# Attention with the keys on partitions, four heads in one product, in a two-layer hybrid trunk

## What is computed

```python
ATT_HEADS, ATT_KV_HEADS, HEAD_DIM, PAST_LEN, DEC_SEQ, SEQ = 8, 2, 64, 256, 1024, 128
# latent tokens see 256 cached keys and the 1024 latent keys; context tokens see their own 128
k_all = concatenate([ctx_k, k]); v_all = concatenate([ctx_v, v])
q = q.reshape(B, T, KV, G, HD) * HEAD_DIM ** -0.5
s = einsum('bqkgd,bskd->bkgqs', qblk, k)
p = softmax(s, axis=-1)
o = einsum('bkgqs,bskd->bqkgd', p, v)
```

## Time and profile before

| | |
|---|---|
| median of three runs | 3227.2 us |
| span of the profiled execution | 3228.9 us |
| latent attention, from its first product to the first of the context stage | 573.6 to 876.8 us |
| context attention, to the first instruction of the output projection | 876.8 to 901.2 us |
| PE busy | 2992.1 us, 93% of the span |
| VectorE, ScalarE, POOL busy | 66%, 39%, 40% |

### The profile page before, as it was taken

One profiled execution on the slowest core, in us unless ns is written; L12 is line 12 of the kernel. 1 busy time (PEld: TensorE's weight loads), 2 busy tenths in 40 slices (PEclk: granted clock), 3 DMA queues, 4 the chain that ended last, 5 costly groups with the idle time before them and its releaser, 6 DMA issues.

```text
span 3228.9 us, 44484 instructions
## 1 busy us (share of the span) xinstructions
PE 2992.1 (93%) x17516; PEld 2613.0 (81%) x17516; DVE 2128.0 (66%) x2691; ACT 1245.2 (39%) x2037; POOL 1278.3 (40%) x851
## 2 busy tenths in 40 slices
PE   7999878999889999999999899959889999999998
PEld 3898657899768999988877888747678999978876
DVE  3689578555467744468796646479777644378886
ACT  2311146555454323233323476544353332233322
POOL 1211036100022544468881221146442544478870
PEclk9999989999989999999999999966799999999999
DMA  5466644100022232243333333242132223232341
GB/s 208 159 248 209 202 134 134 37 25 1 11 98 92 74 111 91 91 140 111 111 114 104 112 116 103 89 126 60 48 103 80 97 91 104 94 131 97 111 170 59
DMA packets 230815, 347.01 MB, mean 107 GB/s; under 512 B 32040, under 2 KB 124240, under 8 KB 230608
## 3 DMA queue, kind: packets, MB, share of 16 engines
q1 hardware_dynamic: 230608, 344.17, 32.0%
HBM read 259.18 MB, written 84.94 MB: 107 GB/s over the span
## 4 chain that ended last, share of the span: by engine, by line
PE 67%; DVE 13%; POOL 10%; issue 4%; ACT 3%; DMA 2%; SPq 1%; POOLq 0%; DVEq 0%; ACTq 0%
PE psum L979 18%; PE psum L1171 9%; PE psum L656 8%; POOL d_slot L1111 5%; PE psum L2462 4%; PE psum L659 4%; PE psum L1276 3%; PE psum L1624 3%; PE psum L2450 2%; PE psum L2457 2%; PE psum L2762 2%; PE psum L1153 2%; DVE mix_x L2945 1%; PE psum L426 1%; PE psum L3689 1%
## 5 line engine op out<-in xcount | busy, mean ns | idle before, releaser
L1171 PE MATMUL psum<-d_slot 128*128 128x512 f32 x2016 | 465.0, 390 | 11.8 <-DVE yacc L1216 6.9
L1171 PEld LDWEIGHTS psum<-d_slot 128*128 128x128 f32 x2016 | 377.5, 188 | 95.0 <-DVE yacc L1216 8.6
L979 PE MATMUL psum<-AT,w_slot 128*128 128x288 f32 x2688 | 366.0, 295 | 4.7 <-POOL w_slot L944 4.7
L979 PEld LDWEIGHTS psum<-AT,w_slot 128*128 128x128 f32 x2688 | 359.5, 188 | 5.1 <-POOL w_slot L944 5.1
L1111 POOL TENSOR_TENSOR d_slot<-down_a,d_slot 128x512 fp32r<-128x512 f32 x168 | 300.4, 1811 | 71.8 <-ACT d_slot L1102 71.6
L591 POOL TENSOR_TENSOR WT<-RAW,WT 128x1024 fp32r<-128x1024 f32 (+3 forms) x34 | 115.1, 3411 | 457.8 <-ACT WT L580 457.8
L656 PE MATMUL psum<-WT,AT 128*128 128x512 f32 (+1 forms) x1296 | 280.6, 377 | 4.2 <-ACT stage L702 4.2
L979 PE MATMUL psum<-s_hi,w_slot 128*128 128x288 f32 x1344 | 269.1, 295 | 5.9 <-issue 4.3
L656 PEld LDWEIGHTS psum<-WT,AT 128*128 128x128 f32 x1296 | 230.6, 189 | 47.1 <-ACT stage L702 4.4
L944 POOL TENSOR_TENSOR w_slot<-RAW,w_slot 128x512 fp32r<-128x512 f32 x112 | 155.8, 1402 | 224.2 <-ACT w_slot L940 224.2
L979 PEld LDWEIGHTS psum<-s_hi,w_slot 128*128 128x128 f32 x1344 | 215.4, 188 | 7.1 <-issue 5.2
(11 more groups left out here) (431 smaller groups left out, 6093.3 us busy)
## 6 DMA issues: line engine op xcount, KB each, us to landing
RAW<-ffn_w SPq DMA_DIRECT2D x40, 1024.0 KB, 6.4
ada_raw<-ada_w SPq DMA_DIRECT2D x36, 1024.0 KB, 6.4
hidden<-hid SPq DMA_DIRECT2D x56, 576.0 KB, 3.3
down_a<-hidden SPq DMA_DIRECT2D x48, 512.0 KB, 6.4
RAW<-ffn_w SPq DMA_DIRECT2D x48, 512.0 KB, 7.8
RAW<-w_in_even SPq DMA_DIRECT2D x5, 2048.0 KB, 8.1
RAW<-w_in_odd SPq DMA_DIRECT2D x5, 2048.0 KB, 7.8
mix_x<-x_all SPq DMA_DIRECT2D x18, 512.0 KB, 3.5
```

What stands on the lines that cost most here:

```text
L979: mm = nc.tensor.matmul(psum[:, bank + b, 0:HB], w_slot[p][:, w, k, :], TOKENS[p][x][:, k, b * HB:(b + 1) * HB], start=(begins and k == 0 ...
L1171: mm = nc.tensor.matmul(psum[:, D_RING[q % 3] + pair % 2, :], slot[:, 0, x, k, pair * P:(pair + 1) * P], slot[:, 1, w, k, :], start=(k == ...
```

## The change

The unit of work becomes a batch: one query tile and the four heads that share a key head, so 16 latent batches and two context ones, and both attention stages become one.

- Row maxima are taken as before, but from scores that leave out the low part of k (`scores`, L2517 of the changed file). The negated maxima are turned and repeated over partitions by a transpose (`turn_maxima`, L2523), and kept in `m_q`, partitions 64 to 127, with the high part of q beside them (POOL, L2683). The low part of `kS` now has a row of ones (and zeros) in its upper half, so that the second product of `turned_scores` adds low k by high q and subtracts the maximum.
- Scores are made again with the keys on partitions (`turned_scores`, L2538 and L2539), two one-pass products of 512 columns (four heads of 128 queries) for each of ten key tiles. ScalarE takes exponentials of those; nothing is turned.
- Values times probabilities (`values`) is 512 columns wide. In four of ten key tiles it is one float32 product (L2556). In six ScalarE takes the exponential twice, into float32 and into fp32r (L2598, L2601), POOL subtracts (L2696), and three one-pass products follow (L2552 to L2554). The values carry 64 columns of ones, so that partitions 64 to 127 of the result are the sums. ScalarE inverts the sums by Ln and Exp (L2608, L2609); VectorE multiplies (`out`).
- `BEHIND` is 2: PE issues the values of step s-2 after the turned scores of step s. A step is one key tile.
- The POOL part of weight group 6 moves to batches 10 to 13, and the loads of the next stage are issued when the last turned scores are done.
- In the mLSTM stage POOL splits only one copy of the low part of k, and there are a few memsets; semaphores are regrouped into three sets.

```diff
@@ mlqk_gpsimd
-                nc.gpsimd.tensor_tensor(hl_k(qk_hl, s, 1), rot_k, hl_k(hlf, s, 0), ALU.subtract).then_inc(qk_split, 1)
+                nc.gpsimd.tensor_tensor(hl_k(qk_hl, s, 1)[:, :, 0, :], qk_rot[:, 8:10, :, :].rearrange("p h c n -> p h (c n)"), hl_k(hlf, s, 0)[:, :, 0, :], ALU.subtract).then_inc(qk_split, 1)
...
+            for s in range(2):
+                for h in (9, 11):
+                    nc.gpsimd.memset(hlf[:, s, h, HD:P], 0.0).then_inc(one_row, 1)
...
@@ att_tensor
-            for n in range(UNITS):
...
-                turn(n, 0, 6)
...
-                    values(n - 1)
...
+            def turned_scores(n, kt):
...
+                if s >= 3:
+                    pe.wait_ge(exp_done, s - 2)
...
+                nc.tensor.matmul(out, kS[:, g, 0, at:at + P], qS[:, g::2, t * P:(t + 1) * P], start=True, stop=False)
+                nc.tensor.matmul(out, kS[:, g, 1, at:at + P], per_head(m_q[:, m_slot(n), :]), start=False, stop=True).then_inc(st_done, 1)
+
+            def values(s):
...
+                pe.wait_ge(exp_done, s + 1)
...
+                if is_split(s):
+                    i, j = SPLIT.index(kt), splits_to(s) % 2
+                    pe.wait_ge(low_done, splits_to(s) + 1)
+                    nc.tensor.matmul(psum[:, o_bank(n), :], values_hl[:, i, g, 0:P], p_high[:, j, :], start=(kt == 0), stop=False)
+                    nc.tensor.matmul(psum[0:HD, o_bank(n), :], values_hl[:, i, g, P:P + HD], p_high[:, j, :], start=False, stop=False, skip_group_check=True)
+                    nc.tensor.matmul(psum[:, o_bank(n), :], values_hl[:, i, g, 0:P], p_low[:, j, :], start=False, stop=False).then_inc(pv_done, 1)
+                    return
...
+                    turned_scores(n, kt)
+                    if n < 2 * CTX - 1:
+                        if kt in (1, 3, 5, 7):
+                            scores(n + 1, kt // 2)
...
+                    if s >= BEHIND:
+                        values(s - BEHIND)
...
+            gate_tensor(pe, 0, 0, diag_att, bank=0)
@@ att_scalar
+            def exponent(s):
+                act.wait_ge(st_done, s + 1)
+                if s >= 3:
+                    act.wait_ge(pv_done, s - 2)
+                if is_split(s):
+                    nc.scalar.activation(prob[:, s % 3, :], psum[:, st_bank(s), :], ACT.Exp)
+                    if splits_to(s) >= 2:
+                        act.wait_ge(pv_done, SPLIT_STEPS[splits_to(s) - 2] + 1)
+                    nc.scalar.activation(p_high[:, splits_to(s) % 2, :], psum[:, st_bank(s), :], ACT.Exp).then_inc(exp_done, 1)
+                    return
...
+                    exponent(steps_to(n) + kt)
+                    if kt == 3 and n:
+                        inverse(n - 1)
+                    if kt == 6 and 4 <= n < 8:
+                        split_high(act, 6, (n - 4, 4))
@@ att_vector
+                    biggest(n, 0)
+                    biggest(n, 1)
+                    if n >= 2:
+                        out(n - 2)
+                    biggest(n, 2)
+                    biggest(n, 3)
@@ att_gpsimd
+                    for kt in SPLIT[:3]:
+                        low(steps_to(n - 1) + kt)
+                copy_queries(n)
+                leave(n - 2)
+                if 10 <= n < 14:
...
+                    ins = nc.gpsimd.tensor_tensor(WT[:, 0, 1, part], RAW[:, part], WTf[:, 0, 0, part], ALU.subtract)
...
+                    for kt in SPLIT[3:]:
+                        low(steps_to(n - 1) + kt)
```

More of the change, by code:

```diff
@@ new lines, in trunk, with batch, key_tiles, steps_to @@
+        BATCHES = 2 * TILES
+        LAST = BATCHES - 1
+        kSf_, qSf = kS[:].bitcast(F32), qS[:].bitcast(F32)
+        per_head = lambda a: a.rearrange("p (j n) -> p j n", j=4)
+        per_pair = lambda a: a.rearrange("p (b r n) -> p b r n", b=2, r=2)
+        def batch(n):
+            return n // 2, n % 2
+        def key_tiles(n):
+            return 1 if n // 2 == CTX else KT
+        def steps_to(n):
+            return sum(key_tiles(m) for m in range(n))
+        def maxima_to(n):
+            return 4 * min(n, 2 * CTX) + max(0, n - 2 * CTX)
@@ new lines, in step_of, with is_split, splits_to @@
+        def step_of(s):
+            n = next(n for n in range(BATCHES) if s < steps_to(n + 1))
+            return n, s - steps_to(n)
+        ALL_STEPS = steps_to(BATCHES)
+        BEHIND = 2
+        SPLIT = [kt for kt in range(KT) if kt % 5 in (0, 2, 3)]
+        WHOLE = [kt for kt in range(KT) if kt not in SPLIT]
+        def is_split(s):
+            n, kt = step_of(s)
+            return n // 2 != CTX and kt in SPLIT
+        SPLIT_STEPS = [s for s in range(ALL_STEPS) if is_split(s)]
+        def splits_to(s):
+            return sum(1 for r in SPLIT_STEPS if r < s)
@@ L3757, in mixer_sync @@
                 att_sync(sp)
-                next_stage(sp, "latent attention")
-                ctx_sync(sp)
-                next_stage(sp, "context attention")
+                next_stage(sp, "attention")
             else:
@@ L3787, in mixer_scalar @@
                 next_stage(act, "mLSTM chunks and norms")
-                att_scalar(act)
-                next_stage(act, "latent attention")
-                ctx_scalar(act)
-                next_stage(act, "context attention")
+                att_scalar(act, chain)
+                next_stage(act, "attention")
             else:
@@ L3819, in mixer_vector @@
                 next_stage(dve, "mLSTM chunks and norms")
-                att_vector(dve, chain)
-                next_stage(dve, "latent attention")
-                ctx_vector(dve, chain)
-                next_stage(dve, "context attention")
+                att_vector(dve)
+                next_stage(dve, "attention")
             else:
```

445 lines of the change are left out of this document (212 added, 233 removed).

## The result

The changed kernel takes 3177.1 us by the median of four runs (3175.9 to 3178.2), against 3228.6 for the kernel before in four (3225.1 to 3231.9). The ratio is 0.9837, with a 95% interval of 0.9825 to 0.9849: 1.6% faster. Between the medians lie 51.5 us. The forecast was 3175.0, within 3158 to 3202. The profiled execution of the changed kernel took 3175.9 with a span of 3174.2.

What follows compares the result with a forecast made beforehand. PE was taken to bound the latent attention. The terms 238 + 3 + 9.5 + 8 + 4 + 6.5 + 7 gave 276 us for what took 327.6, saving 52 from 3227.2: 3175 us, range 3158 to 3202.

Steps and rivals of the forecast that it cites:

- Batches in steady state: Sixteen latent batches: PE work of 14.9 us each, 238 us, plus 0.2 us lost a batch, 3 us.
- The path of the split steps: From turned score over ScalarE and POOL to values: 2.9 us, against 2.7 to 3.6 us of PE cover.
- Weight pieces: POOL's four pieces of weight group 6, batches 10 to 13: each lands nearly whole on PE, 9.5 us, ends 4 to 12.
- Start and clock: Stage start: 8 us before turned scores can flow, and 4 us for PE work at half clock until 586 to 590.
- Context batches and end: Two context batches with a wait for the result bank, 6.5 us, then 7 us of gate tail to the barrier.
- mLSTM stage: Extra semaphore clears and memsets, a narrower low part of k: nothing to half a microsecond either way.
- After the stage: Behind the attention stage nothing was counted; the saving of 52 us was taken from the median of 3227.2.
- The signs: Traces to check: batches 15.0 to 15.2 us, four 17.4; PE waits on `p_low`; wrong if products start over 0.23 apart.
- The split path: Rival, split steps in the batches: with POOL's subtraction at 1.8 us their path ends last, 3202 us; chance 0.10.
- Slower than before: Rival, split steps: POOL takes 2.27 us for each subtraction, 57 us over the sum, 3239 us; chance 0.04.
- Dearer products: Rival, PE's wide products: turned scores 0.25 and float32 records 0.53 us apart, 20 us more, 3195 us; chance 0.10.
- Full cover: Rival, whole stage: hand-overs free, weight pieces half price, gate tail 5.5 us; 13 us less, 3162 us; chance 0.12.

Runs made afterwards that it cites:

- the gate experiment: Changed kernel with the gate row's diagonals, products and copies moved ahead at the attention stage's end; 3175.5 us in total, its tail 10.66 us against 15.23.

## Why the prediction was right, point by point

The sum was 276 us for the stage; it is 273.7. Term by term the misses are +0.6 in the batches, -2.3 at the weight pieces, -3.6 at start and clock, and +2.9 at the end. That the total of 3175 lies 2 us from the measured one owes something to their cancelling, and to where the stage happened to begin.

- **Batches in steady state** (238 + 3 = 241): right. A batch takes 15.0 where 14.9 + 0.2 was forecast, and the sixteen with the first scores make 241.6 us without pieces and start. The surcharge of 0.2 had the wrong reason. PE loses nothing to waits between 588 and 700 us; the tenth over the sum is in the spacing of products, 0.23 to 0.234 for 0.229.
- **The path of the split steps**: "covered by a hair" is shown by three runs: one step less of cover costs 70.8 us, half a microsecond more of POOL 24.5, 1.35 us more 77.6. The path was sized at 2.9 us; the two exponentials take 1.09, not 1.25, so it is 2.7 to 2.8. The thinnest cover was put at 2.7 and is 2.9 (key tile 8, from 655.19 to 658.10). Of the two tiles named as thinnest, 8 is; 7 has 0.5 us and more to spare.
- **Weight pieces** (9.5, ends 4 to 12): the mechanism was right and the size too big, 7.2, since the piece finds 0.5 us of slack ahead of the fourth low part, which the prediction named and didn't subtract.
- **Start and clock** (12): over by 3.6. The first turned score came 9.4 us after the stage's begin (9 forecast), which is 7.1 beyond the scores counted in the batches. The clock was full from 587 on, as forecast, but the half clock added only 1.3 us to the first batch in place of 4. In the run whose clock rose about 3 us after the first turned score instead of 5.8 (the gate experiment) the first batch took 15.4, and the sixteen took 0.9 us less: a microsecond at half clock costs there about 0.3.
- **Context batches and end** (13.5): under by 2.9; 16.4 us. The forecast took the gate row as two short hand-overs. In fact VectorE makes the last two diagonals behind the last division, PE waits 3.4 us for them and then works at half clock, 3.78 us for four records as before. The run with another order and the same work is 4.6 us shorter, 2.8 by the order and 1.8 by the clock, which the forecast had in neither number.
- **mLSTM stage** (nothing to 0.5): nothing can be told, the stage's begin varies by 6 us among kernels that are equal up to there.
- **After the stage**: 0.9 us lost in the profiled executions, as good as the nothing that was forecast. The saving of 52 was taken from the median; the medians differ by 51.5.
- **The signs.** Batches of 15.0 us (16.8 with a piece, 17.4 forecast), POOL at 1.28 and the clock full by 590 came as named. PE was to wait on `p_low` in the steady state too; it does so only behind the pieces. Two signs of being wrong were touched: one-pass products start up to 0.234 us apart, not 0.23, which is the tenth a batch above, and the clock did fall to half inside the stage, in its last six microseconds, at the price just given.

**The rivals.** The split path at 1.8 us of subtraction was priced at 3202; the kernel with 1.8 us took 3202.5. That is close by luck: its batches take 16.3 where the rival had 16.6, its stage 298.1 where the rival had 303, and the stage began 4 us later than in the changed kernel's profile. What didn't come about is the rival's condition: here POOL takes 1.26 to 1.30 us every time. Slower than before needs 2.2 us by the prediction; by a line between the two measured points (24.5 at 1.8, 77.6 at 2.63) the saving of 51.5 is used up at 2.22, and 2.27 gives 3232, 7 under the rival's 3239. Point and price were placed well, as far as a line through two points can tell; what was missing was the slow subtraction. Dearer products: 0.23 and 0.43 apart, neither the strided reading of `qS` nor float32 costs more. Full cover was half true: no waits in steady state, but weight pieces (7.2 for its 4.8) and an end that cost more than it assumed. Its price was also summed wrongly: 3 for the waits, half of 9.5 for the pieces and 1.5 at the end make 9 us less, so 3166 and not 3162. Of the rule that would have made one-pass products of 512 columns 216 ns apart (the Trainium skill, "TensorE: Matmul & The Clock Gate", section "Back-to-back issue gap"): here each brings its own weight load and they are 0.23 apart; the 10 us that the rule promised didn't come.

## What to carry to other kernels

Price a wide rewrite by its parts before crediting the part that names it: of 54 us the splitting into one-pass products brought 8, and one run that leaves it out tells so. An engine that is busy for 60% of a stage can be near its limit when its instructions lie between two products of the busy engine. What counts is the path's length against the cover (here 0.1 to 0.2 us are left), and a long piece in that engine's queue lands on the busy engine; cut to the length of the gaps and put into them, it costs nothing here. More distance between producer and consumer helps only as far as the buffers reach; beyond that it delays the release. And when a new order saves time near a place where the clock falls, look at the granted clock in both traces before giving all of it to the order.

## What the runs showed of the hardware

VectorE with two operands in SBUF and GpSimd exclude each other by whole instructions wherever these traces show them overlap, in both directions: 0.44 us of wait for VectorE, 0.4 for GpSimd in the runs above. The output projection of the changed kernel has the same, and larger:

```profile
856.94 2.29 DVE L3035 TENSOR_TENSOR WT<-RAW,WT 128x2048 fp32r<-128x2048 f32 x1 [2.35 <-ACT WT L581]
859.15 0.68 DVE L3003 TENSOR_TENSOR AT<-psum,AT 128x512 fp32r<-128x512 f32 x1
859.75 4.47 DVE L2988 TENSOR_TENSOR mo_sq<-h_sum 128x512 f32<-128x512 f32 x1
...
856.99 6.69 POOL L2963 TENSOR_TENSOR WT<-RAW,WT 128x2048 fp32r<-128x2048 f32 x1 [4.26 <-ACT WT L581]
```

POOL's piece starts 0.05 us after VectorE's and lasts 6.69, which is VectorE's 2.24 and 4.45 of its own (2.37 for 1024 columns gives 4.6). VectorE's next square, 0.69 us elsewhere, comes in during it and takes 4.47: it ends at 864.22, 0.54 after POOL's. The Trainium skill ("SBUF — State Buffer", "Who interferes with whom") says that these two kinds of instruction contend, and that whoever is first holds the ports for its whole instruction in VectorE's two-port modes; here `tensor_tensor` behaves so as well. Between VectorE's piece and its square, L3003 with one operand in PSUM takes its usual 0.68 us in the midst of POOL's piece. The rule would explain why L1111 takes 1.8 and 2.27 us in the MLP, but only by argument, as no run touched that.

In the sixteen batches VectorE has no instruction with two tensors in SBUF, its maxima, copies and divisions read PSUM, and POOL's subtraction keeps to 1.28 us. The change rests on that: with the 2.27 us that `RAW` brings in the MLP the gain would be gone, by the line above.
